# Five start pieces with four accumulators in turn, and one more half of the first output projection's weights split within the attention, in a two-layer transformer step on one core

## The chip, the cores and the metric

The kernel runs on one NeuronCore of a Trainium2 chip. What counts is the device time of one execution, in microseconds (us). Only the work on the chip is timed; the host lays the weights out beforehand.

## The reference, cut to what matters

The program is one streaming step of a two-layer decoder: 256 prompt rows and 64 sample rows, model width 1024, everything in float32. The change touches the very beginning (the norm and input projection of the first feed-forward half) and the output projection `w_out` of the first layer's attention.

```python
def rms_norm(x, g):
    y = x * lax.rsqrt(jnp.mean(x * x, axis=-1, keepdims=True) + EPS)
    return y * g

def macaron_half(x, g, w_in, w_out):                 # w_in: 1024 x 5632, w_out: 2816 x 1024
    a, b = jnp.split(rms_norm(x, g) @ w_in, 2, axis=-1)
    return x + 0.5 * ((jax.nn.silu(a) * b) @ w_out)

def diff_layer(x, ...):
    x = macaron_half(x, g_ffn1, w_ffn1_in, w_ffn1_out)   # stages in0, out0
    ...                                                  # q, k, v: stage pa
    pm = softmax(q @ k * SCALE + bias)                   # two softmaxes of each of 6 heads
    o = rms_norm((pm[0] - lam * pm[1]) @ v, g_sub)
    om = softmax(qm @ km * SCALE) @ vm                   # memory attention, 4 heads
    x = x + concat(o, om) @ w_out                        # stage wo0
    x = macaron_half(x, g_ffn2, w_ffn2_in, w_ffn2_out)   # stages in1, out1
```

The second layer has the same parts with another attention, and its stages are not touched.

## The kernel before, in words

**Layout.** Activations are kept transposed: 128 partitions of the width, times 320 columns (all rows of prompt and sample). `x`, `xhi` and `xlo` are eight such tiles (k = 0 to 7). Every float32 product is made of three matmuls in the faster format float32r: weights and inputs are each split in a high part (a rounding copy, on ScalarE, ACT) and a low part (the difference, on VectorE, DVE). `product` issues for each k the three matmuls of lines 490 to 492: high by high, high by low input, low weight by high.

**Weights.** They stream through two slots. `raw[s]` is filled by a DMA on SyncE's queue (SP), `whi[s]` is made of it on ACT (`split_hi`) and `wlo[s]` on DVE (`split_lo`); a whole slot is 128x2048 floats, 1 MB, and holds two column tiles of 128 for all eight k. A slot's `raw` may be loaded again after its `wlo` is made (semaphore `lo_ready[s]`), and `whi` and `wlo` may be written again after TensorE (PE) has finished with the slot (`acc_ready`).

**Stage in0.** 22 blocks of weights, taken as 11 pairs: slot 0 holds two tiles of the gate part, slot 1 two tiles of the up part. A pair's four results go to `banks[0]` to `banks[3]` in PSUM. DVE multiplies them by the norm factor `r` into `gate` and `up` and so frees the banks (`acc_free`); ACT makes `silu`; DVE `hid`; ACT `hhi`; DVE `hlo`. The norm factor is not needed before that: the sum of squares (`sq8`, `ssum`) goes through one matmul (`row_norm`, line 500), four operations on ACT and two on DVE.

**The beginning** (lines 410 to 421, 1397 to 1428 and 1895 to 1935). PE first runs 19 matmuls on zeroed data (line 962). The inputs and the first block arrive in four pieces each, of two k: `x` and `raw[0]` in turn, then four pieces of `raw[1]`. PE's `first_pieces` takes slot 0 through all four pieces (both columns), then slot 1 through all four. ACT and DVE split `x` and slot 0 piece by piece, then slot 1, the squares between them. The third block (slot 0 of pair 1) is split in two halves; the second half's `wlo` is made between the two gates of pair 0 (`third`). After pair 0, `memory_in(0)` makes eight tiles of `memhi` on ACT and `memlo` on DVE, ahead of the gates of pair 1. The order on each engine is written out by hand; each engine works strictly in it.

**GpSimd (POOL)** issues five loads of constants, 1 MB in all, as soon as the second block (slot 1 of pair 0) has landed. ACT waits for these constants at the first `hhi` (`settle`), PE at a small matmul `biases` after the second tile of pair 1, which writes `banks[4]`.

**Attention of layer 0.** Nine units: six heads (`diff`, i = 0 to 5) and three of memory attention (i = 6 to 8). PE, ACT, DVE and POOL hand the units to each other; `run_heads_first` is written out for each engine. In each unit PE turns the exponentials (`turns_of`), makes the scores of unit i + 2, and then the values; ACT makes exponentials (`exps`) and one copy of the turned ones (`copy_first`), DVE the other (`copy_second`), the maxima and the inverses. `HALF_AT` says after which unit a half of wo0's weights is split by `split_half`: half 0 at i = 3, half 1 at i = 4 (slot 0). Halves 2 and 3 (slot 1) are split at the end, after the six tiles `sub_scale` and `sub_tiles_hi`. `mix_out` then runs: two column tiles on slot 0 while these splits are made, then the tiles of slot 1.

## Time and profile before

| | us |
|---|---|
| median of 3 runs (1280.08 to 1280.53) | 1280.23 |
| the profiled execution | 1280.21 |
| its span in the trace | 1278.4 |
| around the span | 1.8 |
| PE busy | 1265.4 |
| DVE busy | 741.6 |
| ACT busy | 561.2 |
| POOL busy | 174.8 |

Times in the trace count from the span's start. A matmul of 320 columns follows the one before it 0.147 us later in steady work, while its own row says 0.31 us, since matmuls are pipelined; so lengths of PE's work are best read from start to start. The trace's time is near the median, so a difference in the trace is taken as a difference in the time.

### The profile page before, as it was taken

Reading aid. Unit: us, or ns where it says so; the run is one execution under the profiler, and the core shown is the slowest. Engines: PE = TensorE matmul, PEld = TensorE weight load, DVE = VectorE, ACT = ScalarE, POOL = GpSimd, SP = SyncE. Lnnn points to the kernel's source line nnn. Section 1 sums busy time; section 2 is a strip of 40 time slices with the busy share of each in tenths; the row PEclk is TensorE's granted clock in tenths of the full one; section 3 lists DMA queues with packets and bytes.
Section 4 is the critical chain, followed back from the end, with each engine's and each line's share of the span. In section 5 each row is a group of like instructions: output and inputs, shape, how many; then the busy total and the mean of one; then the engine's idle time right before and its main releaser. Section 6 shows DMA issues by size and latency. Waiting matters only on the chain.

```text
span 1278.4 us, 22446 instructions
## 1 busy us (share of the span) xinstructions
PE 1265.4 (99%) x8784; PEld 1243.9 (97%) x8784; DVE 741.6 (58%) x1128; ACT 561.2 (44%) x827; POOL 174.8 (14%) x208
## 2 busy tenths in 40 slices
PE   9999999999999999999999999999999999999999
PEld 8999999999998999999999999999997899999999
DVE  7756574555677656554454675554446756656433
ACT  7534363353275533333343453433345763343322
POOL 0300020046143100000122000000124510000000
PEclk9999999999999999999999999999999999999999
DMA  8454445553203444444443533454451144343443
GB/s 279 163 160 150 161 139 174 195 188 132 100 34 130 164 151 145 160 163 139 151 164 123 196 133 138 157 164 160 135 187 34 55 144 159 137 164 131 135 140 128
DMA packets 39661, 187.45 MB, mean 147 GB/s; under 512 B 4369, under 2 KB 14353, under 8 KB 24497
## 3 DMA queue, kind: packets, MB, share of 16 engines
q1 hardware_dynamic: 38272, 183.38, 41.8%
q0 software_dynamic: 1184, 3.13, 1.1%
q8 instruction: 42, 0.69, 0.2%
q10 hardware_dynamic: 144, 0.11, 0.0%
q14 instruction: 19, 0.15, 0.0%
HBM read 179.70 MB, written 6.90 MB: 146 GB/s over the span
## 4 chain that ended last, share of the span: by engine, by line
PE 95%; DVE 2%; ACT 1%; issue 1%; DMA 1%; SPq 0%; ACTq 0%; DVEq 0%
PE bank L490 29%; PE bank L492 29%; PE bank L491 29%; PE bank L752 1%; PE bank L713 1%; PE bank L890 1%; PE bank L755 1%; PE bank L722 1%; DVE wlo L1526 1%; DMA raw<-in_w_ffn_in 1%; ACT whi L1120 0%; PE outs L516 0%; ACT ew L1281 0%; PE outs L518 0%; PE outs L500 0%
## 5 line engine op out<-in xcount | busy, mean ns | idle before, releaser
L490 PE MATMUL bank<-xhi,whi 128*128 128x320 f32 (+1 forms) x1760 | 545.8, 310 | 3.0 <-DVE wlo L1901 1.1
L492 PE MATMUL bank<-xhi,wlo 128*128 128x320 f32 (+1 forms) x1760 | 543.0, 309 | 0.0
L491 PE MATMUL bank<-xlo,whi 128*128 128x320 f32 (+1 forms) x1760 | 543.0, 309 | 0.0
L1526 DVE TENSOR_TENSOR wlo<-raw,whi 128x2048 fp32r<-128x2048 f32 (+1 forms) x177 | 364.1, 2057 | 230.2 <-ACT whi L1120 230.1
L1120 ACT ACTIVATE whi<-raw 128x2048 fp32r<-128x2048 f32 (+1 forms) x177 | 304.1, 1718 | 242.3 <-PE bank L492 237.9
L490 PEld LDWEIGHTS bank<-xhi,whi 128*128 128x128 f32 x1760 | 330.5, 188 | 6.2 <-issue 3.4
L491 PEld LDWEIGHTS bank<-xlo,whi 128*128 128x128 f32 x1760 | 330.6, 188 | 0.5
L492 PEld LDWEIGHTS bank<-xhi,wlo 128*128 128x128 f32 x1760 | 330.5, 188 | 0.0
L490 PE MATMUL bank<-hhi,whi 128*128 128x320 f32 x704 | 219.0, 311 | 0.0
L492 PE MATMUL bank<-hhi,wlo 128*128 128x320 f32 x704 | 217.5, 309 | 0.0
L491 PE MATMUL bank<-hlo,whi 128*128 128x320 f32 x704 | 217.5, 309 | 0.0
L490 PEld LDWEIGHTS bank<-hhi,whi 128*128 128x128 f32 x704 | 132.2, 188 | 2.4 <-DVE wlo L1526 2.1
L491 PEld LDWEIGHTS bank<-hlo,whi 128*128 128x128 f32 x704 | 132.2, 188 | 0.0
L492 PEld LDWEIGHTS bank<-hhi,wlo 128*128 128x128 f32 x704 | 132.2, 188 | 0.0
L1217 ACT ACTIVATE hhi<-hid 128x320 f32 (+1 forms) x88 | 40.8, 463 | 134.0 <-DVE hid L1653 134.0
L1209 ACT ACTIVATE silu<-gate 128x320 f32<-128x320 f32 x88 | 40.8, 463 | 107.0 <-DVE gate L1643 106.6
L1643 DVE TENSOR_TENSOR gate<-bank,r 128x320 f32<-128x320 f32 x88 | 42.7, 488 | 73.9 <-PE bank L492 73.4
L2103 POOL TENSOR_TENSOR ssum<-ssum,sq 128x320 f32<-128x320 f32 (+1 forms) x42 | 39.2, 933 | 231.6 <-ACT sq L1245 188.0
L1659 DVE TENSOR_TENSOR hlo<-hid,hhi 128x320 f32 (+1 forms) x88 | 43.7, 497 | 29.7 <-ACT hhi L1217 29.7
L1650 DVE TENSOR_TENSOR up<-bank,r 128x320 f32<-128x320 f32 x88 | 42.9, 487 | 25.8 <-PE bank L492 25.8
L1242 ACT ACTIVATE xhi<-x,early 128x320 fp32r<-128x320 f32 (+1 forms) x24 | 13.5, 564 | 99.6 <-DVE x L1684 99.6
L2118 POOL TENSOR_TENSOR hsq_lo<-hsq,hsq_hi 128x320 fp32r<-128x320 f32 (+1 forms) x38 | 52.7, 1387 | 19.2 <-ACT hsq_hi L1162 17.7
(233 smaller groups left out, 1041.5 us busy)
## 6 DMA issues: line engine op xcount, KB each, us to landing
raw<-in_w_ffn_in SPq DMA_DIRECT2D x86, 1024.0 KB, 4.8
raw<-in_w_ffn_out SPq DMA_DIRECT2D x64, 704.0 KB, 4.2
raw<-in_w_in_a SPq DMA_DIRECT2D x10, 1024.0 KB, 4.8
raw<-in_w_out SPq DMA_DIRECT2D x8, 1024.0 KB, 4.9
raw<-in_w_kv SPq DMA_DIRECT2D x6, 1024.0 KB, 4.8
raw<-in_w_mkv SPq DMA_DIRECT2D x4, 1024.0 KB, 4.7
raw<-in_w_in_b SPq DMA_DIRECT2D x4, 1024.0 KB, 4.7
raw<-in_w_ffn_in SPq DMA_DIRECT2D x8, 256.0 KB, 7.2
```

Of the source, the lines that this page charges most:

```text
L490: mm(acc, wh, mhi(ks[q]), start=start and q == 0, stop=False)
L491: mm(acc, wh, mlo(ks[q]), start=False, stop=False)
L492: last = mm(acc, wl, mhi(ks[q]), start=False, stop=stop and q == nk - 1)
L1120: nc.scalar.activation(whi[slot][:, 0:size], raw[slot][:, 0:size], ACT.Copy).then_inc(hi_ready[slot], 1)
L1209: nc.scalar.activation(silu[:, c, :], gate[:, c, :], ACT.Silu).then_inc(silu_out, 1)
L1217: nc.scalar.activation(hhi[:, bass.ds(2 * i + c, 1), :], hid[:, c:c + 1, :], ACT.Copy).then_inc(hh_ready, 1)
L1526: tt(wlo[slot][:, 0:size], raw[slot][:, 0:size], f32(whi[slot][:, 0:size]), ALU.subtract).then_inc(lo_ready[slot], 1)
L1643: tt(gate[:, c, :], banks[c][:, 0:R], r[:], ALU.mult).then_inc(acc_free, 1)
L1650: tt(up[:, c, :], banks[2 + c][:, 0:R], r[:], ALU.mult).then_inc(acc_free, 1)
L1659: tt(hlo[:, bass.ds(2 * i + c, 1), :], hid[:, c:c + 1, :], f32(hhi[:, bass.ds(2 * i + c, 1), :]), ALU.subtract).then_inc(hl_ready, 1)
L2103: nc.gpsimd.tensor_tensor(ssum[:, 0:w], ssum[:, 0:w], sq[:, k % 2, 0:w], ALU.add).then_inc(ssum_step, 1)
L2118: nc.gpsimd.tensor_tensor(hsq_lo[:, s % 2, 0:w], hsq[:, 0:w], hsq_hi[:, s % 2, 0:w].bitcast(F32), ALU.subtract).then_inc(hlo_ready, 1)
```

## The change

1. **Start pieces.** `START` makes five pieces out of four: k = 0; k = 1; k = 2, 3; k = 4, 5; k = 6, 7. For each piece `x`, slot 0's weights and slot 1's weights are loaded one after the other. Slot 1's first piece is issued from ACT's queue.
2. **Four accumulators in turn.** PE goes through the pieces, and for each piece through both slots, so that all four tiles grow together. `row_norm` stands in the last piece, ahead of its slot 1. There are 15 matmuls on zeroed data in place of 19. ACT and DVE split both slots piece by piece; all squares and their sum come after the pieces.
3. **The third and fourth block.** The third block is loaded in two halves, the first one as soon as slot 0's third piece is split. Both halves are split ahead of the norm's operations on DVE (before: one ahead of them, one between the gates), and the fourth block, 128x2048, is split right after the norm's operations, ahead of pair 0's gates (before: after pair 0's second `hid`).
4. **Spare banks.** Pair 1's first two tiles go to `banks[4]` and `banks[5]`, without waiting for a free bank; DVE reads them there. `biases` moves to the bank `HS`.
5. **POOL's constants** wait for the third block (`landed[0]` at 32) instead of the second.
6. **Half 2 of wo0** is split after unit i = 5, ahead of unit 6's copies, on ACT and on DVE; half 3 stays at the end.

The diff, cut to its core:

```diff
-HALF_AT = {3: 0, 4: 1}
+START = [(0, 1), (1, 2), (2, 4), (4, 6), (6, 8)]
+LAST = len(START) - 1
+HALF_AT = {3: 0, 4: 1, 5: 2}
...
@@ SyncE @@
+            for q, (k0, k1) in enumerate(START):
+                own = slice(256 * k0, 256 * k1)
+                sp.dma_start(x[:, k0:k1], x_v[:, k0:k1]).then_inc(d_x[q], 16)
+                sp.dma_start(raw[0][:, own], weights["in0"][0][:, own]
+                             ).then_inc(d_piece[q] if q < LAST else landed[0], 16)
+                if q:
+                    sp.dma_start(raw[1][:, own], weights["in0"][1][:, own]
+                                 ).then_inc(d_piece1[q] if q < LAST else landed[1], 16)
+            sp.wait_ge(piece_lo, 3)
+            sp.dma_start(raw[0][:, 0:BLK // 2], weights["in0"][2][:, 0:BLK // 2]).then_inc(d_third, 16)
+            sp.wait_ge(lo_ready[0], 1)
+            sp.dma_start(raw[0][:, BLK // 2:BLK], weights["in0"][2][:, BLK // 2:BLK]).then_inc(landed[0], 16)
+            sp.wait_ge(lo_ready[1], 1)
+            sp.dma_start(raw[1][:], weights["in0"][3]).then_inc(landed[1], 16)
...
@@ TensorE @@
+                    for q, (k0, k1) in enumerate(START):
+                        pe.wait_ge(xn_lo, k1)
+                        for slot, some in ((0, piece_lo), (1, piece1_lo)):
+                            if q == LAST:
+                                pe.wait_ge(lo_ready[slot], 1)
+                                if slot == 1:
+                                    row_norm(stage, R)
+                            else:
+                                pe.wait_ge(some, q + 1)
+                            for col in range(2):
+                                last = product(..., part=range(k0, k1))
+                                if q == LAST:
+                                    last.then_inc(acc_ready, 1)
+                            if slot == 0 and k1 == KD // 2:
+                                last.then_inc(first_half, 1)
...
-                        wait_acc(t0 + 4 * i + j)
+                        spare = halves and j < 2
+                        if not spare:
+                            wait_acc(t0 + 4 * i + j)
...
-            for _ in range(19):
+            for _ in range(15):
...
@@ ScalarE @@
-                        if c == 1:
+                        if c == 1 and not (stage == "in0" and isinstance(i, int) and i == 0):
                             split_hi(1, n0 + i + 1, ...)
...
-                    split_half("wo0", 2)
                     split_half("wo0", 3)
...
+            for k in range(KD):
+                nc.scalar.activation(sq8[:, k, :], x[:, k, :], ACT.Square).then_inc(sq_ready, 1)
+            act.wait_ge(d_third, 16)
+            act.wait_ge(first_half, 1)
+            nc.scalar.activation(whi[0][:, 0:BLK // 2], raw[0][:, 0:BLK // 2], ACT.Copy).then_inc(third_hi, 1)
             act.wait_ge(landed[0], 16 * (PAIR0["in0"] + 1) + 16)
             act.wait_ge(acc_ready, TILE0["in0"] + 2)
+            nc.scalar.activation(whi[0][:, BLK // 2:BLK], raw[0][:, BLK // 2:BLK], ACT.Copy).then_inc(hi_ready[0], 1)
             row_norm("in0", R)
+            split_hi(1, PAIR0["in0"] + 1, BLK, acc_ready, TILE0["in0"] + 4)
...
@@ VectorE @@
             dve.wait_ge(third_hi, 1)
             tt(wlo[0][:, 0:BLK // 2], ...).then_inc(third_lo, 1)
+            dve.wait_ge(hi_ready[0], PAIR0["in0"] + 2)
+            tt(wlo[0][:, BLK // 2:BLK], ...).then_inc(lo_ready[0], 1)
             row_norm("in0", R)
+            split_lo(1, PAIR0["in0"] + 1, BLK)
...
-                            split_half("wo0", 2)
                             split_half("wo0", 3)
...
@@ GpSimd @@
-            pool.wait_ge(landed[1], 16)
+            pool.wait_ge(landed[0], 32)
```

What stands in a row on DVE from the third block's first half (first line) to pair 0's first `hid`, before:

```order
L1927 TENSOR_TENSOR wlo<-raw,whi 128x1024
L1547 SCALAR_TENSOR_TENSOR rt<-outs,rt 128x320
L1553 SCALAR_TENSOR_TENSOR r<-rt 128x320
L1643 TENSOR_TENSOR gate<-bank,r 128x320
L1934 TENSOR_TENSOR wlo<-raw,whi 128x1024
L1643 TENSOR_TENSOR gate<-bank,r 128x320
L1650 TENSOR_TENSOR up<-bank,r 128x320
L1653 TENSOR_TENSOR hid<-up,silu 128x320
```

The same stretch of DVE in the changed kernel:

```order
L1930 TENSOR_TENSOR wlo<-raw,whi 128x1024
L1933 TENSOR_TENSOR wlo<-raw,whi 128x1024
L1560 SCALAR_TENSOR_TENSOR rt<-outs,rt 128x320
L1566 SCALAR_TENSOR_TENSOR r<-rt 128x320
L1539 TENSOR_TENSOR wlo<-raw,whi 128x2048
L1657 TENSOR_TENSOR gate<-bank,r 128x320 x2
L1664 TENSOR_TENSOR up<-bank,r 128x320
L1667 TENSOR_TENSOR hid<-up,silu 128x320
```

The second half and the whole fourth block now stand ahead of the first gate.

On ACT the same place, from the third block's first half to pair 0's last `hhi`, before:

```order
L1426 ACTIVATE whi<-raw 128x1024
L1137 ACTIVATE rt<-outs,early 128x320
L1139 ACTIVATE rt<-rt 128x320
L1141 ACTIVATE rt<-rt 128x320
L1142 ACTIVATE rt<-rt 128x320
L1428 ACTIVATE whi<-raw 128x1024
L1204 ACT_TABLE_LOAD
L1209 ACTIVATE silu<-gate 128x320 x2
L1217 ACTIVATE hhi<-hid 128x320
L1120 ACTIVATE whi<-raw 128x2048
L1217 ACTIVATE hhi<-hid 128x320
```

And in the changed kernel:

```order
L1436 ACTIVATE whi<-raw 128x1024
L1439 ACTIVATE whi<-raw 128x1024
L1157 ACTIVATE rt<-outs,early 128x320
L1159 ACTIVATE rt<-rt 128x320
L1161 ACTIVATE rt<-rt 128x320
L1162 ACTIVATE rt<-rt 128x320
L1140 ACTIVATE whi<-raw 128x2048
L1224 ACT_TABLE_LOAD
L1229 ACTIVATE silu<-gate 128x320 x2
L1237 ACTIVATE hhi<-hid 128x320 x2
```

The second half stands ahead of the norm's four operations, and the fourth block right behind them, ahead of the table load and both `silu`.

On DVE at the end of the sixth unit (i = 5): its last maximum (ISA), its output tile (`qk<-outs`), and then unit 6's copy of the turned exponentials (`pt<-bank`), before:

```order
L1737 ISA ew,nb<-bank,late 128x256
L1737 ISA nb 128x1
L1795 COPY qk<-outs 128x320
L1784 COPY pt<-bank 128x256
L1750 RECIPROCAL rc<-sm 128x2
```

In the changed kernel:

```order
L1751 ISA ew,nb<-bank,late 128x256
L1751 ISA nb 128x1
L1809 COPY qk<-outs 128x320
L1549 TENSOR_TENSOR wlo<-raw,whi 128x1024
L1798 COPY pt<-bank 128x256
L1764 RECIPROCAL rc<-sm 128x2
```

Half 2's low part stands between the output tile and the next unit's copy.

## Rows read from the trace of the kernel before

**Rows 1.** The page: busy time, share and instructions of each engine.

```profile
PE 1265.4 (99%) x8784; PEld 1243.9 (97%) x8784; DVE 741.6 (58%) x1128; ACT 561.2 (44%) x827; POOL 174.8 (14%) x208
```

**Rows 2.** Timeline to 15 us: start, length, engine, line, operation, idle before and releaser.

```profile
1.25 5.41 PE L962 MATMUL bank<-mixhi 128*128 128x320 f32 x19 [1.25 <-DVE mixhi L1891]
...
4.50 1.01 ACT L1166 ACTIVATE xhi<-x,early 128x320 fp32r<-128x320 f32 x2 [2.01 <-DMA x<-in_xT]
...
7.20 0.38 PE L490 MATMUL bank<-xhi,whi 128*128 128x320 f32 x1 [0.53 <-issue]
...
8.90 0.63 ACT L1405 ACTIVATE whi<-raw 128x512 fp32r<-128x512 f32 x1 [1.28 <-DMA raw<-in_w_ffn_in]
...
9.74 1.02 ACT L1166 ACTIVATE xhi<-x,early 128x320 fp32r<-128x320 f32 x2 [0.21 <-DMA x<-in_xT]
...
10.31 0.42 PE L490 MATMUL bank<-xhi,whi 128*128 128x320 f32 x1 [1.13 <-DVE wlo L1901]
...
14.86 0.76 POOL L2211 DMA_DIRECT2D select<-in_select  x1 [14.42 <-DMA raw<-in_w_ffn_in]
```

**Rows 3.** Timeline, 16 to 28 us: the norm, pair 0's first gate, the third and fourth block.

```profile
16.42 2.28 DVE L1909 TENSOR_TENSOR ssum<-ssum,sq 128x320 f32<-128x320 f32 x4
...
19.97 0.53 ACT L1137 ACTIVATE rt<-outs,early 128x320 f32<-128x320 f32 x1 [0.16 <-PE outs L500]
...
21.77 1.04 ACT L1428 ACTIVATE whi<-raw 128x1024 fp32r<-128x1024 f32 x1
...
22.59 0.49 DVE L1643 TENSOR_TENSOR gate<-bank,r 128x320 f32<-128x320 f32 x1
...
23.00 1.22 DVE L1934 TENSOR_TENSOR wlo<-raw,whi 128x1024 fp32r<-128x1024 f32 x1
...
23.28 0.31 PE L490 MATMUL bank<-xhi,whi 128*128 128x320 f32 x1
...
25.95 1.90 ACT L1120 ACTIVATE whi<-raw 128x2048 fp32r<-128x2048 f32 x1
...
27.88 2.29 DVE L1526 TENSOR_TENSOR wlo<-raw,whi 128x2048 fp32r<-128x2048 f32 x1 [0.38 <-ACT whi L1120]
```

**Rows 4.** Timeline, 30 to 39 us: pair 1, and the start of pair 2.

```profile
30.49 3.25 DVE L1603 SCALAR_TENSOR_TENSOR memlo<-memt,early,memhi 128x256 fp32r<-128x256 f32 x8
...
36.48 2.29 DVE L1526 TENSOR_TENSOR wlo<-raw,whi 128x2048 fp32r<-128x2048 f32 x1 [1.94 <-ACT whi L1120]
...
38.15 0.31 PE L492 MATMUL bank<-xhi,wlo 128*128 128x320 f32 x1
...
38.91 0.41 PE L490 MATMUL bank<-xhi,whi 128*128 128x320 f32 x1 [0.46 <-DVE wlo L1526]
```

**Rows 5.** Timeline of DVE, ACT, POOL and PE, units 4 to 8 of the attention.

```profile
377.12 1.70 DVE L1536 TENSOR_TENSOR wlo<-raw,whi 128x1024 fp32r<-128x1024 f32 x1 [0.19 <-ACT whi L1129]
...
378.80 0.38 ACT L1291 ACTIVATE pt<-bank 128x256 f32<-128x256 f32 x1 [1.22 <-PE bank L752]
...
382.42 0.42 DVE L1784 COPY pt<-bank 128x256 f32<-128x256 f32 x1 [0.30 <-PE bank L755]
...
381.64 0.49 ACT L1281 ACTIVATE ew<-ew,nb 128x256 f32<-128x256 f32 x1
...
377.03 0.72 POOL L2113 TENSOR_TENSOR hsq<-qk 128x320 f32<-128x320 f32 x1
...
382.21 0.72 POOL L2113 TENSOR_TENSOR hsq<-qk 128x320 f32<-128x320 f32 x1 [0.49 <-DVE qk L1795]
...
390.20 1.08 PE L782 MATMUL outs<-pt,vm 128*64 128x256 f32 x8 [1.27 <-ACT pt L1291]
```

**Rows 6.** Timeline, 396 to 401 us: the last halves of wo0 and the first matmul on them.

```profile
396.49 3.62 DVE L1536 TENSOR_TENSOR wlo<-raw,whi 128x1024 fp32r<-128x1024 f32 x2 [1.49 <-ACT whi L1129]
...
397.18 2.46 PE L890 MATMUL bank<-mixlo,whi 128*128 128x320 f32 x14
...
400.16 0.41 PE L490 MATMUL bank<-mixhi,whi 128*128 128x320 f32 x1 [0.52 <-DVE wlo L1536]
```

More of the change, by code:

```diff
@@ L349, in encoder_kernel @@
         d_mem = sem("d_mem")
-        d_piece = [sem(f"d_piece{q}") for q in range(3)]
-        d_piece1 = [sem(f"d_piece1{q}") for q in range(3)]
+        d_piece = [sem(f"d_piece{q}") for q in range(LAST)]
+        d_piece1 = [sem(f"d_piece1{q}") for q in range(LAST)]
         piece1_hi = sem("piece1_hi")
         ones_there = sem("ones_there")
+        d_third = sem("d_third")
+        first_half = sem("first_half")
         third_hi = sem("third_hi")
@@ L364, in encoder_kernel @@
         d_early = sem("d_early")
-        d_x = [sem(f"d_x{q}") for q in range(4)]
+        d_x = [sem(f"d_x{q}") for q in range(LAST + 1)]
         d_const = sem("d_const")
@@ L587, in first_pieces @@
                 def first_pieces():
-                    for slot, some, all_ in ((0, piece_lo, lo_ready[0]), (1, piece1_lo, lo_ready[1])):
-                        for q in range(4):
-                            if slot == 1 and q == 2:
-                                row_norm(stage, R)
-                            pe.wait_ge(all_, 1) if q == 3 else pe.wait_ge(some, q + 1)
-                            if slot == 0:
-                                pe.wait_ge(xn_lo, 2 * q + 2)
+                    for q, (k0, k1) in enumerate(START):
[7 more added lines that the diff above has]
+                                pe.wait_ge(some, q + 1)
                             for col in range(2):
@@ L618, in each @@
                                 pe.wait_ge(xn_lo, x0 + k + 1)
-                        product(banks[j][:, 0:R], slot, col, 256, range(KD), KD,
+                        product(banks[4 + j if spare else j][:, 0:R], slot, col, 256, range(KD), KD,
                                 lambda k: xhi[:, k, :], lambda k: xlo[:, k, :], True, True, each
@@ L966, in biases @@
                 pe.wait_ge(d_const, CONST)
-                mm(banks[4][0:H_A, 0:NREL + 1], table[:], hot[:], start=True, stop=True).then_inc(trel_ready, 1)
+                mm(HS[0:H_A, 0:NREL + 1], table[:], hot[:], start=True, stop=True).then_inc(trel_ready, 1)
             def stats_mkv0(j):
@@ L1397, in _ @@
             act.dma_start(early[:], a["early"]).then_inc(d_early, 16)
+            act.dma_start(raw[1][:, 0:256], weights["in0"][1][:, 0:256]).then_inc(d_piece1[0], 16)
             nc.scalar.preload_act_table_set("natural_log_exp_and_others")
             act.wait_ge(d_early, 16)
-            for q in range(4):
+            for q, (k0, k1) in enumerate(START):
+                own = slice(256 * k0, 256 * k1)
                 act.wait_ge(d_x[q], 16)
-                for k in (2 * q, 2 * q + 1):
+                for k in range(k0, k1):
@@ L1403, in _ @@
                     input_hi(x[:, k, :], xhi[:, k, :], "ffn1_0", k)
-                act.wait_ge(d_piece[q] if q < 3 else landed[0], 16)
-                nc.scalar.activation(whi[0][:, 512 * q:512 * (q + 1)], raw[0][:, 512 * q:512 * (q + 1)], ACT.Copy
-                                     ).then_inc(piece_hi if q < 3 else hi_ready[0], 1)
-            def squares(tiles):
-                for k in tiles:
-                    nc.scalar.activation(sq8[:, k, :], x[:, k, :], ACT.Square).then_inc(sq_ready, 1)
@@ L1412, in piece1 @@
-            def piece1(q):
-                act.wait_ge(d_piece1[q] if q < 3 else landed[1], 16)
-                nc.scalar.activation(whi[1][:, 512 * q:512 * (q + 1)], raw[1][:, 512 * q:512 * (q + 1)], ACT.Copy
-                                     ).then_inc(piece1_hi if q < 3 else hi_ready[1], 1)
-            piece1(0)
-            squares(range(4))
-            piece1(1)
-            squares(range(4, KD))
-            piece1(2)
-            piece1(3)
+                act.wait_ge(d_piece[q] if q < LAST else landed[0], 16)
@@ L1640, in body @@
                 def body(i, size, at=None):
+                    spare = stage == "in0" and isinstance(i, int) and i == 1
                     for c in range(2):
                         dve.wait_ge(acc_ready, t0 + 4 * i + c + 1)
-                        tt(gate[:, c, :], banks[c][:, 0:R], r[:], ALU.mult).then_inc(acc_free, 1)
+                        tt(gate[:, c, :], banks[4 + c if spare else c][:, 0:R], r[:], ALU.mult).then_inc(acc_free, 1)
                         if at:
@@ L1655, in body @@
                             at(2 + c)
-                        if c == 1:
+                        if c == 1 and not (stage == "in0" and isinstance(i, int) and i == 0):
                             split_lo(1, n0 + i + 1, size)
@@ L1663, in ffn_in @@
                     for i in range(3):
-                        body(i, BLK, third if stage == "in0" and i == 0 else None)
+                        body(i, BLK)
                         after(i)
@@ L1894, in _ @@
             nc.vector.memset(f32(lf8_lo[:]), 0.0)
-            for q in range(4):
-                inputs_lo("in0", "ffn1_0", lambda k: x[:, k, :], R, tiles=(2 * q, 2 * q + 1))
-                if q < 3:
+            for q, (k0, k1) in enumerate(START):
+                own = slice(256 * k0, 256 * k1)
+                inputs_lo("in0", "ffn1_0", lambda k: x[:, k, :], R, tiles=range(k0, k1))
+                if q < LAST:
                     dve.wait_ge(piece_hi, q + 1)
```

57 lines of the change are left out of this document (20 added, 37 removed).

## The prediction

> **What bounds the kernel now.** First the page: PE is busy 1265.4 us of a span of 1278.4 us, 99% [rows 1]. No edit of order can bring more than the rest, some 13 us, and this one touches only two places. So I read the timeline there for the moments at which PE starts late, and from start to start. At the beginning: the first product starts at 7.20, the next piece's at 10.31, after about 1.3 us without work (12 matmuls at 0.147 us end the steady part near 9.0) [rows 2]. Pair 1 starts at 23.28 [rows 3]. Pair 2 starts at 38.91, released by DVE's `wlo`, where 38.30 (38.15 plus one step of 0.147) would have been steady: 0.6 us lost [rows 4]. At the first output projection: the tiles on slot 1 start at 400.16; 14 matmuls that should take 2.05 us started at 397.18, and the next start is 2.98 us later, so PE lost 0.25 us among them (it takes the `mixlo` tiles of POOL) and 0.68 us after them, at DVE's `wlo` [rows 6]. These waits, 1.3, 0.6, 0.25 and 0.68, and the start at 7.20, are all that the change can win.
>
> **Part 1, the first piece.** What has landed when, in bytes: the first pieces of `early` and `x` (425 KB) by 4.5; x and slot 0 up to k = 3 (1257 KB) by 8.9; the third piece of x (1577 KB) by 9.7; everything (3433 KB) by 14.8, when POOL is released [rows 2]. From 8.9 on that is 2176 KB in 5.8 us, 375 KB per us. The order of the bytes changes, their sum hardly. The new first piece (265 KB to its x, 521 KB to the weights of both slots) I put at 3.9 and 4.9, between the rows for 425 KB and 1257 KB. A 512-wide high part takes 0.63 [rows 2]; a half block, 1024 wide, takes 1.04 on ACT and 1.22 on DVE [rows 3]; so a 256-wide part is some 0.4 on either, and the low part of 512 some 0.65. First product: 4.9 + 0.4 + 0.4 + 0.1 = 5.8, 1.4 earlier than 7.20. Two pieces are 24 matmuls, 3.5 us, so PE is through at 9.3. It then waits for piece three: its x is at 1257 KB, thus 8.9; two `xhi` 1.0, the high part 0.55, the low part 0.6 and two handovers 0.15: 11.2. PE loses 1.9 us instead of 1.3.
>
> From 11.2 on nothing waits: pieces four and five (3177 KB at 14.0, 3433 KB at 14.8) are split by 16.2, and PE needs the fifth's slot 0 at 18.3. 72 matmuls are 10.6 us, the norm's matmul costs 0.7 of PE. The sum of squares now comes wholly after the pieces: eight squares from 15.4, adds of 0.57 each [rows 3] from 16.2 to 20.1, needed at 20.0, so 0.2 us more. Pair 1 starts at 11.2 + 10.6 + 0.7 + 0.2 = 22.7, 0.6 us earlier than 23.28 [rows 3].
>
> **Part 2, the fourth block ahead of the gates.** Before, DVE's first gate is at 22.59, in the same moment as the norm factor [rows 3]. Now: PE is through with slot 0 of pair 0 after 60 matmuls, 11.2 + 8.8 = 20.0. ACT then splits the second half (1.0, to 21.1), runs the norm's four operations (1.8, from 19.97 to 21.77 before [rows 3]; to 22.9), then the fourth block's high part (1.9; to 24.8), and DVE its low part (2.3) [rows 3]. The first gate is at 27.1, 4.5 us later than before. The spare banks keep PE going through pair 1 meanwhile, and its third tile needs a bank only at 30.6, freed by 28.4. But pair 2's weights hang on this chain too: their high part stands on ACT behind `silu` of pair 1, that behind pair 1's gate, and that behind pair 0's work and eight `memlo` (3.25 us, 30.49) [rows 4]. From the first gate to pair 2's first product it was 38.91 - 22.59 = 16.32 us. Of these, the half split (1.22) and the whole one (2.29) leave the stretch, less some 0.1 each by which rows overlap what follows: 13.0 are left [rows 3, 4]. Pair 2 starts at 27.1 + 13.0 = 40.1. PE is ready at 22.7 + 15.0 (before, 23.28 to 38.30) = 37.7, and waits 2.4 us. **Net +1.2 us** against 38.91. Bounds: -1.2 if the chain does not bind (37.7); +0.5 if piece three lands 1.7 us sooner, since the fourth piece then bounds; +2.2 if all pieces land 1 us later. After pair 2 nothing is carried on: a pair takes PE 14.1 us and DVE about 9.
>
> POOL's constants now start at 19.3 (the second half of the third block, issued at 15.6) instead of 14.86. ACT needs them at 28.9, PE at 29.7. They landed within 8 us of 14.86 or PE's use of them would have been late; by 27.3 is in time. Cost nothing; with under 1.6 us to spare.
>
> **Part 3, half 2 in the sixth unit.** At the end both halves took DVE 3.62 us; now one, 1.81, starting behind ACT's first. It is done before PE comes: the 0.68 us go, and I count 0.25 for `mixlo`, for which POOL competes with DVE there [rows 6]. What it costs: ACT can start its high part when unit 7's exponentials of the first bank are through, 381.64, and needs 1.0; DVE starts the low part at 382.7 and holds it 1.2 us or more. Behind it stands unit 6's copy, which ran at 382.42 with only 0.30 us of idle time ahead, and behind that the inverses and maxima without a break. In unit 4 the same split (377.12 to 378.82) cost nothing, since the next copies, released at 378.80, waited for PE anyway. Here PE itself waits at the end of the chain, 1.3 us before 390.20, for ACT's copy [rows 5]. So DVE's delay goes through to 390.20 in full: 382.7 + 1.16 - 382.42 = 1.45 alone.
>
> How long DVE holds it depends on POOL. Splits of a half took 1.22 alone [rows 3], 1.70 at 377.12 beside a product of POOL of 0.72 from 377.03 [rows 5], and 1.81 each at the end [rows 6]. The same product now starts at 382.21 and ends at 382.93, over the start of the new split: 0.2 more, 1.6 in all. (The Trainium skill, page "SBUF — State Buffer", section "Who interferes with whom", says that a DVE instruction with two SBUF inputs and a GpSimd instruction that reads SBUF exclude each other for the whole instruction, the first to issue going ahead. By that rule the split would wait to 382.93, and the delay would be 1.67; without it, 1.45. The rows 377.03 and 377.12 agree with it: 0.63 of overlap, 0.48 longer.) **Net +1.6 - 0.9 = +0.7 us**; bounds -0.9 (delay hidden) and +1.1 (1.8 of delay, no gain on `mixlo`).
>
> **The sum.** 1280.21 (the profiled execution, level with the median 1280.23) + 1.2 + 0.7 = 1282.1.
>
> **The rivals.**
> - *It does what it says.* The gates come early enough, pair 2 starts at 37.7, and half 2 hides: -1.2 - 0.9, 1278.1. For it: PE's earlier start and the gap at 400.16 are real. Against: the two chains above, neither of which has slack in the rows. 5%.
> - *Only the sixth unit hides* (PE's wait before 390.20 swallows it): +1.2 - 0.9, 1280.5. 13%.
> - *Only the start goes well*: -1.2 + 0.7, 1279.7. 10%.
> - *The pieces land late.* 14 small loads on SP and one on ACT stand where 12 stood; the last x piece is at 2921 KB instead of 2153 KB. If the stream from piece three on runs 1 us behind my line, PE's third piece, the norm and the chain to pair 2 all slip by that 1 us: 1283.1. From 0.7 us on, the kernel is slower than can be called the same. For it: between 425 and 1257 KB the rows show only 190 KB per us. 22%.
> - *The clock.* The 19 warm-up matmuls took 5.41 us, 0.285 each: the 1.2 GHz level; the products from 7.20 on run at 2.4 GHz [rows 2]. There are 15 now, and a wait of 1.9 us comes after 3.5 us of work. If PE falls back to the lower level at 11.2 for some 24 matmuls, that is 3.3 us: 1285.4. Against: a wait of 1.3 us after 1.8 us of work did not do it. 5%.
>
> **How the numbers follow.** The forecast, 1281.2 to 1282.8, has 45%. What a measurement can tell from no change is about 0.2%, 2.6 us: 1277.7 to 1282.8. Faster than that is hardly anything even if all goes well: 3%. Slower: late pieces, the clock, and the upper edge of the forecast: 28%. Within: 69%. The range 1278.9 to 1284.2 leaves out the first rival and the clock, and some 5% of the rest on either side.
>
> **What would show it.** Right: first product near 5.8; a PE wait of near 2 us before piece three; pair 1 near 22.7; DVE's first gate near 27.1; PE idle 2.4 us before pair 2, released by DVE's `wlo`, at 40.1; unit 6's copy 1.6 us later against the products around it; no wait at the first product on slot 1 of wo0. Wrong: pair 2 starts without a wait, or the first gate stands before 25; the wait before ACT's last copy (390.20) shrinks by what half 2 takes; the matmuls after 11.2 stand 0.27 us apart; `hhi` of pair 0 waits for constants.

## The result, and the profile after

The changed kernel takes 1288.05 us (median of 4 runs, 1286.86 to 1288.32); the kernel before, beside it, 1280.21. The ratio is 1.006, 95% interval 1.0047 to 1.0073: slower by 7.8 us, where the forecast was 1282.1 and the range ended at 1284.2. The profiled execution took 1287.83, its span is 1285.8 against 1278.4. Three of the four executions have a mean granted clock of 0.997, the fourth 0.999, and that one is the shortest by 1.0 to 1.5 us. One execution of the half alone below, 1361.82 us at a mean clock of 0.851, is a slow one and stands in none of the figures.

Read in the order of the forecast, the start first. These rows are the timeline of the changed kernel (start, length, engine, line, operation, idle time before and what ended it).

```profile
5.42 0.60 PE L503 MATMUL bank<-xhi,whi 128*128 128x320 f32 x1
...
10.41 0.38 PE L503 MATMUL bank<-xhi,whi 128*128 128x320 f32 x1 [0.41 <-DVE wlo L1915]
...
20.19 0.76 POOL L2212 DMA_DIRECT2D select<-in_select  x1 [19.74 <-DMA raw<-in_w_ffn_in]
...
23.06 1.92 ACT L1140 ACTIVATE whi<-raw 128x2048 fp32r<-128x2048 f32 x1 [0.32 <-DMA raw<-in_w_ffn_in]
...
27.29 0.88 DVE L1657 TENSOR_TENSOR gate<-bank,r 128x320 f32<-128x320 f32 x2
...
30.48 0.81 PE L987 MATMUL outs<-hot,table 32*6 32x384 f32 x2 [0.93 <-DMA lamv<-in_lamv]
...
30.52 0.47 ACT L1237 ACTIVATE hhi<-hid 128x320 fp32r<-128x320 f32 x1 [1.84 <-DMA lamv<-in_lamv]
...
39.41 2.29 DVE L1539 TENSOR_TENSOR wlo<-raw,whi 128x2048 fp32r<-128x2048 f32 x1 [1.94 <-ACT whi L1140]
...
41.84 0.63 PE L503 MATMUL bank<-xhi,whi 128*128 128x320 f32 x1 [3.32 <-DVE wlo L1539]
```

The first product stands at 5.42 (before, 7.20 [rows 2]); the next piece at 10.41 (10.31 before). Pair 1 starts at 22.35 (23.28 [rows 3]). The first gate is at 27.29 (22.59 [rows 3]). New is the row at 30.52: pair 0's first `hhi` waited 1.84 us, and what ended the wait is `lamv`, the last of POOL's constants. From the first gate to pair 2 it is 14.55 us instead of 13.0, and pair 2 starts at 41.84 (38.91 [rows 4]), after PE's last matmul before it had started at 38.22.

The windows view by stretch (length, each engine's busy time and instructions, PE's granted clock as a share of 2.4 GHz, DMA's share, GB/s) adds what no row of a matmul says by itself. First the changed kernel, then the kernel before:

```profile
22.35:41.36 19.01, 15.24 (x100) 14.07 (x98) 12.79 (x22) 11.24 (x19) 0.75 (x2) 1.00 0.52 188
...
41.36:44.77 3.41, 2.92 (x11) 2.93 (x12) 2.62 (x6) 2.11 (x2) 0.00 (x0) 0.50 0.49 151
...
392.93:396.34 3.41, 3.12 (x14) 2.06 (x15) 2.74 (x10) 2.74 (x9) 0.00 (x0) 0.50 0.00 0
```

```profile
41.36:44.77 3.41, 3.41 (x26) 3.41 (x25) 3.02 (x3) 1.77 (x5) 1.88 (x2) 1.00 0.56 228
```

Twice the clock fell to its lower level (0.50, 1.2 GHz), once at 41.36, within the wait before pair 2, so that PE came out of it at the lower level. Eleven matmuls began in the 2.93 us from 41.84 on, where the steady 0.147 us would have brought 20: 1.3 us lost. Behind it the changed kernel is 4.25 us late (PE's start after its wait near 182 against 178 in the kernel before), and 4.47 at the beginning of the attention.

The attention, the timeline of the changed kernel again:

```profile
386.69 0.72 POOL L2114 TENSOR_TENSOR hsq<-qk 128x320 f32<-128x320 f32 x1 [0.49 <-DVE qk L1809]
...
387.20 1.29 DVE L1549 TENSOR_TENSOR wlo<-raw,whi 128x1024 fp32r<-128x1024 f32 x1 [0.60 <-ACT whi L1149]
...
388.41 0.41 DVE L1798 COPY pt<-bank 128x256 f32<-128x256 f32 x1
...
388.93 0.69 PE L796 MATMUL outs<-pt,cmv 128*64 128x64 f32 x16 [0.33 <-issue]
...
388.93 1.29 DVE L1772 TENSOR_SCALAR ew<-ew,rc 128x256 f32<-128x256 f32 x2
...
388.95 0.86 POOL L2119 TENSOR_TENSOR hsq_lo<-hsq,hsq_hi 128x320 fp32r<-128x320 f32 x1 [1.54 <-ACT hsq_hi L1182]
...
390.27 0.66 PE L775 MATMUL bank<-early,ew 128*128 128x128 f32 x4 [0.66 <-DVE ew L1772]
...
393.22 1.97 PE L802 MATMUL outs<-pt,vm 128*64 128x256 f32 x8 [0.58 <-DVE pt L1798]
...
398.01 1.08 PE L802 MATMUL outs<-pt,vm 128*64 128x256 f32 x8 [1.22 <-ACT pt L1311]
...
404.30 1.81 DVE L1549 TENSOR_TENSOR wlo<-raw,whi 128x1024 fp32r<-128x1024 f32 x1 [1.49 <-ACT whi L1149]
...
407.31 0.31 PE L503 MATMUL bank<-mixhi,whi 128*128 128x320 f32 x1
```

The same pair of scalings on DVE in the kernel before:

```profile
382.95 0.62 DVE L1758 TENSOR_SCALAR ew<-ew,rc 128x256 f32<-128x256 f32 x2
```

Unit 6's copy stands at 388.41; before it was at 382.42 [rows 5], and with the 4.47 carried in that is 1.52 later. Behind it DVE's two scalings take 1.29 instead of 0.62, another 0.67. Then the second low-clock stretch lies over the values of the eighth unit (i = 7), 1.97 for eight matmuls that take 1.08 otherwise. PE's last start in this chain is at 398.01, before 390.20 [rows 5]: 7.81 later, so the attention lost 3.34. The first product on slot 1 starts at 407.31 without a wait, 7.15 later than 400.16 [rows 6]: 0.66 is given back, and the end is 7.3 later.

### The profile page after: what moved, and what is told of

The parts are those of the page before. It is cut to its first block, busy times and chain, and to the rows that moved or that the text cites. A ratio compares the mean times of both kernels' runs of the same rounds, so it can differ in the third digit from the quotient of the medians.

```text
span 1285.8 us, 22448 instructions
## 1 busy us (share of the span) xinstructions
PE 1268.4 (99%) x8780; PEld 1245.8 (97%) x8780; DVE 742.3 (58%) x1130; ACT 561.7 (44%) x829; POOL 174.8 (14%) x208
## 4 chain that ended last, share of the span: by engine, by line
PE 93%; DVE 3%; ACT 1%; DMA 1%; issue 1%; SPq 0%; POOL 0%; ACTq 0%; DVEq 0%
PE bank L503 29%; PE bank L505 28%; PE bank L504 28%; PE bank L910 1%; PE bank L772 1%; PE bank L733 1%; DMA lamv<-in_lamv 1%; PE bank L775 1%; PE bank L742 1%; DVE wlo L1539 1%; DMA x<-in_xT 0%; DVE xlo L1616 0%; ACT whi L1140 0%; PE outs L802 0%; PE outs L529 0%
```

## The experiments

The kernels ran on four chips, each of them beside runs of the kernel before on the same chip (medians of it 1279.2 to 1279.5); the ratios are to those. Five questions were put: which part costs what; what the constants wait for; what the wait before pair 2 stands on; what the low clock costs; what the half in the attention costs.

### The two parts apart

The start alone is the changed kernel with half 2 back at the end:

```diff
-HALF_AT = {3: 0, 4: 1, 5: 2}
+HALF_AT = {3: 0, 4: 1}
...
+                    split_half("wo0", 2)
                     split_half("wo0", 3)
```

> The changed kernel without its last part: halves 2 and 3 of the first output projection's weights are both split at the end again. My theory: the two parts cost apart, some 4.5 us at the start and some 2.7 us in the attention (net of the 0.7 us that the removed wait gives back), so this is at 1284.7 to 1285.5 us, with pair 2 at about 41.9 us as in the changed kernel and the attention as before, at the high clock. Rival: the attention's low-clock stretch comes from the shifted or shorter start and not from half 2: then the clock is low again near 393 us and the time is above 1286.

The half alone is the kernel before with the same lines the other way round.

> The kernel before with the last part alone: half 2 is split after the sixth unit. My theory: DVE's copy of unit 6 is 1.5 us later, the scaling of unit 7 another 0.7 us if it meets POOL again, and the tiles on slot 1 start without a wait: 1281.7 us if the clock stays high in the attention, 1282.9 if it falls there. Rival: the cost came from the late start; then the unit hides the split and the time is 1279.5 to 1280.3.

Start alone: 1285.26, ratio 1.0044 (1.0030 to 1.0058). Half alone: 1281.35, ratio 1.0014 (1.0004 to 1.0024). Over the 1279.3 beside them that is 6.0 and 2.1, together 8.0 against the 7.8 of the whole: the parts add up, in the total. In the traces of the first comparison the start had cost less (4.5) and the rest more (2.9), so the two differences partly cancel. The start alone has its constants, its wait and its low clock at the same places as the whole, and no low clock in the attention (first fence: start alone); the half alone has the wait before pair 2 of the kernel before, and the low clock in the attention (second fence, timeline and windows of the half alone).

```profile
30.81 0.47 ACT L1237 ACTIVATE hhi<-hid 128x320 fp32r<-128x320 f32 x1 [2.05 <-DMA lamv<-in_lamv]
...
42.13 0.63 PE L503 MATMUL bank<-xhi,whi 128*128 128x320 f32 x1 [3.32 <-DVE wlo L1540]
```

```profile
37.57 0.41 PE L490 MATMUL bank<-xhi,whi 128*128 128x320 f32 x1 [0.45 <-DVE wlo L1525]
...
386.08:389.50 3.42, 3.12 (x14) 1.74 (x12) 2.79 (x12) 2.70 (x10) 0.00 (x0) 0.50 0.00 0
```

The two rows of pair 2 come from one chip, and differ by 4.56 us, not by the 2.93 of the first comparison. The start of the kernel before had pair 2 at 37.57 here and at 38.91 in the rows on which the forecast rests; its median is 1 us lower here too. Its first gate stands at 21.25 here, and between 21.25 and 21.55 in all four later traces with that start, where the first trace had 22.59: the one trace used for the forecast was a late one. The changed kernel did not become quicker with it (42.13 and 41.84).

### What the constants wait for

POOL's constants back to an earlier moment:

```diff
-            pool.wait_ge(landed[0], 32)
+            pool.wait_ge(landed[1], 16)
```

> The changed kernel, but POOL issues its constants when the second block has landed (at 14.2 us), as before. My theory: ACT's first high part of the hidden tile no longer waits 1.8 us, the biases do not wait, pair 2 starts at 40.2 to 40.4 instead of 41.85, and if PE's wait of about 2 us is too short for the clock to fall, 1.3 us more come back: 1285.1 to 1286.5. Rival: the constants only took their turn in the DMA queues, so the third and fourth block and the memory inputs become late in their place and pair 2 stays at 41.5 or later: 1287.5 and above.

1288.42, ratio 1.0069: nothing gained. `hhi` no longer waits for them, but the third block's second half came for ACT at 22.71 instead of 19.90, and pair 2 started at 43.09:

```profile
22.71 1.06 ACT L1439 ACTIVATE whi<-raw 128x1024 fp32r<-128x1024 f32 x1 [3.70 <-DMA raw<-in_w_ffn_in]
```

So the constants take their time from the weights, and putting them first moves the wait. The fourth block's split put back in its old place, behind pair 0's second `hid`:

```diff
-                        if c == 1 and not (stage == "in0" and isinstance(i, int) and i == 0):
+                        if c == 1:
                             split_hi(1, n0 + i + 1, ...)
...
-            split_hi(1, PAIR0["in0"] + 1, BLK, acc_ready, TILE0["in0"] + 4)
```

(and the same on DVE.)

> The changed kernel, but the fourth block is split in its old place, behind pair 0's second hidden tile, on ACT and DVE; the gates come right after the norm factor, near 23.4. My theory: the late constants (30.4 us) then bind alone, since the fourth block's low part now stands behind them on DVE: it is ready near 34.9, PE waits some 3.7 us in pair 1 and again before pair 2, which starts near 43.9; 1289 to 1290.5, slower than the changed kernel. Rival: the place of the split is the whole cost of the start; then pair 2 starts before 39 and the time is below 1285.5.

1288.64, ratio 1.0070. `hhi` now came to its place 3.7 us sooner, waited 5.56 us, and started no earlier, at 30.84; the fourth block behind it came late for PE:

```profile
30.84 0.47 ACT L1237 ACTIVATE hhi<-hid 128x320 fp32r<-128x320 f32 x1 [5.56 <-DMA lamv<-in_lamv]
...
35.49 0.64 PE L503 MATMUL bank<-xhi,whi 128*128 128x320 f32 x1 [3.88 <-DVE wlo L1538]
```

The constants, not the gates, were what bound there. Which loads they share the stream with was still open. SyncE issues the memory inputs (`memt`, 1 MB) right after the fourth block; in the start alone they are now held back until the constants are in:

```diff
+            sp.wait_ge(d_const, CONST)
             sp.dma_start(memt[:], a["memT"] ...)
```

> The start alone (both halves at the end), and SyncE sends the memory inputs only when POOL's constants have landed. My theory: the constants were late (30.4 to 30.7 us) because they shared the DMA engines with 1 MB of memory inputs; now they land before 28.5, the hidden tile's first high part does not wait, and pair 2 starts at 40.2 to 40.8 instead of 42.1; PE's wait is near 2 us; with the clock still falling 1284, without 1282.8. Rival: the constants' landing is POOL's own pace of making descriptors; then they land near 30 all the same, the memory inputs and the next block come even later and the time is 1286 or more.

1283.95, ratio 1.0038 (1.0024 to 1.0052), 0.8 us below the start alone by the ratios, whose intervals overlap, and 1.1 in the traces (pair 2 at 40.99 instead of 42.13). The constants landed near 26.2 instead of 30.7, and `hhi` waits for DVE's `hid` only; the memory inputs came at 31.95, and ACT waited 0.39 us for them. SyncE issues in order, so the edit held back not one load but two: the fifth block, 1 MB as well, stands behind the memory inputs. In the changed kernel the two are issued at 16.13 and 22.42 (first fence; the second line holds the fifth block and the one after it), here at 26.19 and 26.92.

```profile
16.13 0.43 SPq L434 DMA_DIRECT2D memt<-in_memT  x1
...
22.42 5.48 SPq L398 DMA_DIRECT2D raw<-in_w_ffn_in  x2
```

```profile
29.16 0.47 ACT L1238 ACTIVATE hhi<-hid 128x320 fp32r<-128x320 f32 x1 [0.45 <-DVE hid L1669]
...
31.98 3.31 ACT L1187 ACTIVATE memhi<-memt,early 128x256 fp32r<-128x256 f32 x8 [0.39 <-DMA memt<-in_memT]
```

Thus shown: the constants were late because SyncE's 1 MB loads ran beside them on another queue; the last constant, `lamv`, took 9.4 us from its issue in the start alone and 3.3 us here, so POOL's own pace, the rival, is out. In the changed kernel the DMA share is 1.00 from 17 to 31 us. How much is due to the memory inputs and how much to the fifth block was not separated. (The Trainium skill, page "DMA: Bandwidth & Descriptors", section "Queues, rings and completion order", says that each DMA engine takes turns among the queues that it has work for, a packet at a time. These landings agree: 26.2 without the two neighbours, 30.7 with them.)

### The memory inputs' split, and where the wait goes

Eight `memhi` on ACT and eight `memlo` on DVE stand between the gate and pair 2. In the start alone they were moved behind pair 1:

```diff
-                if i == 0:
+                if i == 0:
+                    return
+                if i == 1:
                     act.wait_ge(d_mem, 16)
```

> The start alone, with the eight high and low parts of the memory inputs one pair later on ACT and DVE (behind pair 1 instead of pair 0). My theory: they are the 3.3 us that lengthen the chain from the first gate to pair 2's weights; pair 2 starts near 38.8, PE waits about 1 us or less, the clock stays high, and the time is 1280.5 to 1282. Rival: pair 2 is bound by its block's landing or by something later; then it starts at 41 or later, or the same wait shows before pair 3.

1283.27, ratio 1.0032 (1.0019 to 1.0044), not the 1280.5 to 1282 expected. The wait before pair 2 is gone, a wait of 1.2 us before pair 3 has come (PE's starts at 54.20 and 55.59, 0.147 of it the step), and the clock was low at 32.13 to 35.55, behind PE's wait for the constants at `biases`. Both edits together:

> The changed start alone (half 2 of the first output projection stays at the old place), with two edits together: the memory inputs' load is issued only when the constants have landed, and both parts of the split of the memory inputs are done one pair later on ACT and DVE. Theory (the start loses by two things only, the constants that land behind the memory inputs, and the memory inputs' split between the gate and pair 2, each with its low-clock stretch behind TensorE's wait): constants land near 26, TensorE's waits near 29.3 and 37.7 are both gone, with them both stretches at clock 0.50, and what is left is the wait before pair 3 near 54, 1.4 us in the run with the later memory inputs. The time is that run's +3.9 over before, less the 1.5 us wait and the 1.7 us of low clock of its trace: +0.7, ratio 1.0005 (1.000 to 1.0015). Rival (a low-clock stretch comes somewhere in the start whenever TensorE began late and high, whatever waits are there): a stretch at 0.50 is seen again, and the ratio is 1.002.

1283.57, ratio 1.0027 (1.0015 to 1.0039), not the 1.0005 expected. Pair 2 starts at 38.69, near its 38.91 in the first trace of the kernel before, and still little is won against either edit alone: the wait before pair 3 is 2.05 us now (PE's starts at 52.72 and 54.92), and a low-clock stretch follows it.

```profile
55.82:59.23 3.41, 3.41 (x15) 3.41 (x14) 2.57 (x4) 3.16 (x5) 0.47 (x1) 0.50 0.85 308
```

The rival of that run was the nearer one. It fits that the work of ACT and DVE in this stretch as a whole is late against PE, and an order only chooses before which pair PE waits; no run with less of that work was made. The kernel before with the memory inputs later was the same question put to the other side:

> The kernel before with one edit: the memory inputs' split one pair later on ACT and DVE. Theory (the 0.5 us that TensorE waits before pair 2 is its doing, and the wait before pair 3 takes its place at least in part): 0 to 0.5 us under the kernel before, ratio 0.9996 to 1.000. Rival (the split meets ACT and DVE at a worse place one pair later, where the third pair's halves are needed): a wait of 1.4 us before pair 3 as in the run of the changed start, ratio 1.0008.

1280.18, ratio 1.0006 (0.9997 to 1.0015). Its wait before pair 2 went, and one of 1.2 us before pair 3 took its place (PE's starts at 51.19 and 52.57). The 0 to 0.5 us expected did not come; it can't be told from no change, and shows no gain.

### What the low clock costs at the start

In the start alone, 20 extra matmuls before pair 2:

```diff
+                    pe.wait_ge(r_ready, 1)
+                    for _ in range(20):
+                        mm(MS[:, 0:R], mixhi[:, 0, 0:P], mixhi[:, 0, :], start=True, stop=True)
                     with pe.Fori(1, 5) as i:
```

> The start alone, with 20 matmuls on zeroed data (2.9 us at the high clock) between pair 1 and pair 2, where PE waits 3.6 us; their result is used by nobody. My theory: the low clock after pair 2's start is the consequence of that wait; with the matmuls the clock stays high, pair 2 still starts near 42 us, and 1.3 us come back: 1284 against 1285.3 of the start alone. Rival: the clock falls for another reason (the start as a whole, the data); then it falls here too, and the time is the same or longer.

1284.25, ratio 1.0037. The test missed: pair 2 came at full clock, but the stretch at 0.50 stood earlier, at 32.00 to 35.42, behind the 1.4 us that PE waited for the constants at `biases`. With that wait gone too (the constants ahead of the memory inputs), the extra matmuls cover the only wait of over 1 us left from 21 to 41 us:

> The changed start alone, memory inputs' load behind the constants, and 20 extra matmuls on finished data just before pair 2, where TensorE waited from 37.70 to 40.99; their result is not used. Since the wait for the constants is gone in this kernel, no other wait of over 1 us lies between 21 and 41. Theory (the low clock at pair 2 is the wait's doing, and costs 1.3 us on top of it): pair 2 starts at 41.0 as without the extra work, no stretch at clock 0.50 in the start, and the time is 1.3 us under that of the same kernel without them: ratio 1.0028 against 1.0038. Rival (the low clock comes whatever TensorE does before pair 2, or moves): a stretch at 0.50 near 32 or 41 and a ratio of 1.0038.

```profile
37.37 3.10 PE L653 MATMUL outs<-mixhi 128*128 128x320 f32 x20
...
20.00:60.00 40.00, 40.00 (x267) 39.00 (x268) 29.83 (x43) 23.58 (x38) 8.36 (x10) 1.00 0.52 189
```

1282.96, ratio 1.0028 (1.0016 to 1.0039). All 7 runs have a mean clock of 1.000, where the 5 runs of the same kernel without extra work have 0.998 or 0.999, and the ratio is 0.0010 lower: the low clock at pair 2 costs 1.0 to 1.3 us on top of the wait that brings it on. The two ratios come from two chips and their intervals overlap, and pair 2 starts at 40.30 here, not at the 41.0 expected, since the first gate of this execution stands 0.5 us earlier than in the one it is compared with (26.84 against 27.32). So the size rests on the count of matmuls above; that the wait brings the low clock on rests on all 7 runs being free of it.

### The half in the attention

Before with half 2 on ACT alone in the sixth unit, its low part at the end of the attention as before:

```diff
+                        if i == 5:
+                            split_half("wo0", 2)
                         if i == 8:
...
-                    split_half("wo0", 2)
                     split_half("wo0", 3)
```

(on ACT only.)

> The kernel before, with half 2's high part made on ACT after the sixth unit, but its low part still on DVE at the end. My theory: the cost of half 2 in the sixth unit is DVE's 1.2 us and what follows on DVE; ACT's 1.0 us alone is hidden or costs under 0.4, and the low parts at the end start 1 to 1.5 us earlier, so that the wait at the first tile of slot 1 goes: 0.2 to 0.9 us faster than before, no low clock. Rival: ACT's copy of unit 6 is what PE waited for; then it costs some 1 us, gives 0.7 back, and the time is the same or up to 1 us slower.

1279.99, ratio 1.0006 (0.9996 to 1.0016), no low clock, and not the gain of 0.2 to 0.9 us expected. PE's last start in the attention came 0.6 us late, though DVE had no split there. ACT's high part alone moved the next operations, and DVE's scalings and POOL's `hsq_lo` met again; at the end the low parts were done by 397.8, and now PE waited for POOL's `mixlo`:

```profile
383.15 1.23 DVE L1759 TENSOR_SCALAR ew<-ew,rc 128x256 f32<-128x256 f32 x2
...
383.25 0.98 POOL L2119 TENSOR_TENSOR hsq_lo<-hsq,hsq_hi 128x320 fp32r<-128x320 f32 x1 [1.53 <-ACT hsq_hi L1162]
...
398.56 0.56 PE L890 MATMUL bank<-mixlo,whi 128*128 128x320 f32 x2 [0.41 <-POOL mixlo L2174]
...
399.39 0.56 PE L890 MATMUL bank<-mixlo,whi 128*128 128x320 f32 x2 [0.27 <-POOL mixlo L2174]
```

(The Trainium skill, page "SBUF — State Buffer", section "Who interferes with whom", says that a DVE instruction in a two-port mode and one of GpSimd exclude each other for the whole instruction, the first to issue going ahead. In both traces the pair of scalings is longer by 0.6 to 0.7 us where it begins together with `hsq_lo`, which agrees; that these scalings run in such a mode no row shows by itself.) No run took `hsq_lo` away from the scalings; that it is the cause rests on five traces in which the pair is 1.2 to 1.3 us with `hsq_lo` beside it, and on the other pairs of the same traces, 0.6 us each without.

The half alone with extra matmuls at its four new waits (before the values of units i = 6 and 7, and before either half of the transpositions of i = 7):

```diff
+                def busy(out):
+                    for _ in range(5):
+                        mm(out, select[:, 0:P], select[:, 0:192], start=True, stop=True)
```

> The kernel before with the half-2 split in the sixth unit (as in the run of the half alone), and 5 extra matmuls on constants in each of four places where TensorE waited in that run (before the values of the seventh and the eighth unit, before either half of the eighth unit's transpositions; waits of 0.72, 0.88, 1.03 and 0.77 us at 382 to 388); their result is not used. Theory (the split costs some 0.9 us by DVE's delays and about 1 us by the stretch at clock 0.50 that the string of waits brings on): no stretch at 0.50 between 380 and 400, the memory unit's matmuls (x8) near 388 take 1.1 us and not 1.97, and the time falls by 1 us, ratio 1.0006 against 1.0014. Rival (the low clock costs nothing, since the work there waits for ACT and DVE anyway): the stretch is gone or not, the ratio stays 1.0014.

1280.98, ratio 1.0013 (1.0004 to 1.0022). Windows and timeline of this run:

```profile
380.00:400.00 20.00, 18.51 (x142) 16.32 (x141) 15.70 (x42) 13.41 (x36) 10.27 (x12) 1.00 0.12 48
...
387.93 1.08 PE L794 MATMUL outs<-pt,vm 128*64 128x256 f32 x8
...
391.42 1.08 PE L794 MATMUL outs<-pt,vm 128*64 128x256 f32 x8 [1.27 <-ACT pt L1303]
```

The stretch is gone and the eight matmuls take 1.08, as the theory said; the ratio stayed where it was, as the rival said. The single runs explain it: of the half alone's, the six with a mean clock of 1.000 have a median of 1280.87, and the three with 0.999 took 1281.39, 1282.59 and 1282.79. So an execution with the low clock is some 0.5 to 1.9 us longer, one in three has it, and the median hardly feels it. DVE's delays are what every execution pays. From PE's first matmul on `select` after its wait near 350 (354.83 in the changed kernel) to its last start after a wait in the attention, it is 39.84 us in the kernel before, 42.00 here, 42.86 in the half alone and 43.18 in the changed kernel: so the delay without low clock is 2.16 (1.5 of the split, 0.67 of the scalings), and 0.9 to 1.2 comes on top with it.

### The whole change, mended

The changed kernel with the constants ahead of the memory inputs and both sets of extra matmuls:

> The whole changed kernel with three edits of the runs before: the memory inputs' load issued once the constants have landed, 20 extra matmuls before pair 2, and the extra matmuls at the four places of the sixth unit's neighbourhood. Theory (the parts add up): 1.0028 of the start so mended, and 1.0006 of the half so mended, less nothing for the wait at slot 1 of the output projection: ratio 1.0034, 4.4 us over the kernel before, against 6 to 7.8 for the change as it is, and no stretch at clock 0.50 at all. Rival (they do not add, a low-clock stretch turns up elsewhere): a stretch at 0.50 in the trace and a ratio of 1.0045 or more.

1284.65, ratio 1.0042 (1.0028 to 1.0056), all runs at a mean clock of 1.000. That is the 1.0028 of the start so mended and the 1.0013 of the half so mended, which add up to 1.0041; the 1.0034 expected took the half too low. Pair 2:

```profile
37.78 3.10 PE L653 MATMUL outs<-mixhi 128*128 128x320 f32 x20
...
41.16 0.41 PE L504 MATMUL bank<-xhi,whi 128*128 128x320 f32 x1 [0.29 <-DVE wlo L1555]
```

It starts at 41.16; on the same chip it is 37.97 in the half alone with extra matmuls, whose start is that of the kernel before. 3.2 us of the 3.7 between those two kernels stand there, the price of the chain from the first gate (27.62 against 21.45) to pair 2. Some 0.5 us more gathers between 180 and 990; its cause stays open. No kernel of this study is faster than the kernel before.

## Why the prediction was wrong

**The first piece** was forecast well: first product 5.8 (5.42), pair 1 at 22.7 (22.35). The wait before piece three was 0.56 us, not 1.9, since the loads came sooner than my line; the norm's sum took 0.5 of that back.

**The gate chain** was right in its mechanism and nearly in its size: first gate 27.1 (27.29), and without the constants' wait 13.2 us from there to pair 2 (14.55 less 1.4; 13.0 from 26.84 to the end of `wlo` at 39.86 in the run with constants first and PE kept busy, and the 0.14 us from there to PE's start). What it is worth depends on when the kernel before comes to pair 2. The one trace used had it at 38.91, three others at 37.57, 37.66 and 37.97, and there the same chain costs 3.0 to 3.2 us instead of 1.5. A single trace could not show that.

**"Cost nothing; with under 1.6 us to spare"** is the step that failed first. I bounded the constants by the 8 us that they took from 14.86, when SyncE's next 1 MB loads were issued 5 us behind them, at 19.93 and 20.30. At their new place, 20.19, the memory inputs are in flight already (issued at 16.13, 12.5 us to landing) and the fifth block is issued 2 us behind, at 22.42; the constants took 10.3 us, to near 30.4. With 8 us they would have been in at 28.2, in time for `hid`, which was ready at 29.1. So `hhi` stood 1.4 us later than `hid` allowed (its idle time of 1.84 holds 0.45 that it waits in the run with constants first too), straight into the chain. The margin had been named, but no rival was made of it.

**The clock rival** had the right mechanism at the wrong place. It was priced at 11.2, behind a wait of 1.9 us, and left out at pair 2, behind a wait that the forecast itself put at 2.4 us and that became 3.3. It fell there, at 1.3 us. With the second stretch, in the attention, the low clock is the largest sum that the forecast lacks, up to 2.5 us.

**The sixth unit.** The delay of the split was 1.52 (forecast 1.6), and the wait at slot 1 went, 0.66 (forecast 0.68). Three sizes were missed: DVE's scalings now begin together with POOL's `hsq_lo`, 0.67; four small waits of PE in a row brought a second low clock, up to 1.2; and the 0.25 for `mixlo` did not come: the 14 matmuls from 404.99 to 407.31 lose 0.27, and POOL's six tiles take 6.05 us as before, even 7.01 where the two splits run earlier beside them. The first of these is the same overlap with POOL as the one that was weighed for the split itself; I weighed it for the moved instruction, and not for the ones behind it.

By the traces: forecast 1.9, constants 1.4, clock at the start 1.3, gate, chain and small waits 0.6, scalings 0.7, clock in the attention 1.2, `mixlo` 0.25: 7.35, where the spans differ by 7.4. The term of the gate and small waits is partly what the others leave over.

## What to carry to other kernels

- A load that is moved has a new neighbour. What it took at its old place is no bound; look at which loads are in flight or are issued within its flight at the new one, on any queue. An edit that holds back one load holds back those behind it on its queue too.
- Wherever a forecast has TensorE wait for longer than before, add the low clock behind it as a term with its own price, about 1.2 us here; it followed one wait of 3 us, one of 1.4 us and a string of 0.7 to 1.0 us waits. A delay of a DVE instruction also moves all that stand behind it against POOL's instructions.
- Look at the start in more than one trace of the kernel before: the only one used here was about 1 us late, and the chain costs 1.5 us against it and 3.0 to 3.2 against the others.
- If ACT and DVE together are late against PE over a whole stretch, moving one piece of their work may only move PE's wait to the next pair, as in the three runs that moved the memory inputs.

## What the runs showed of the hardware

- The same five loads of POOL, 1 MB in all, were in 8 us after the first was issued at 14.86, and 10.3 us after it when issued at 20.19; with the memory inputs and the fifth block held back, in 5.6 us, near 26.2 (6.6 in the run with PE kept busy, 18.78 to 25.38).
- The clock fell behind waits much shorter than the one before pair 2: in the run with the memory inputs later, PE waited from 29.32 to 30.86 and the level was 0.50 from 32.13 to 35.55; before pair 3, a wait of 2.05 us, and 0.50 from 55.82. A wait of 1.1 us at the same matmul in the changed kernel (starts at 29.24 and 30.48) brought none, nor did the waits of 1.3 us at 8.9 and near 389 in the kernel before. The executions of one kernel differ in it: three of nine in the half alone, and one of 18 of the kernel before beside the runs with constants first (1282.55 at a mean clock of 0.999, where their median is 1279.2).
- Two scalings of DVE together, 0.62 us alone, took 1.29 and 1.23 where they began within 0.1 us of an operation of POOL of 0.86 to 0.98.
